# Sending 1536 columns of the upper 64 rows of one weight chunk to the lower partitions

## The reference, cut to what matters

```python
def _expert_choice_ffn(h, w_router, b_router, w_gate, w_up, w_down):
    ...
    gate, idx = lax.top_k(jnp.swapaxes(aff, 1, 2), cap)          # cap = 32 tokens for each of 16 experts
    xs = jax.vmap(lambda hb, ib: hb[ib])(h, idx)
    a = jnp.einsum('becd,edf->becf', xs, w_gate)                 # 1024 -> 2048
    u = jnp.einsum('becd,edf->becf', xs, w_up)                   # 1024 -> 2048
    y = jnp.einsum('becf,efd->becd', jax.nn.silu(a) * u, w_down) * gate[..., None].astype(h.dtype)
    ...                                                          # 2048 -> 1024, rows added back to their tokens
```

## Time and profile before

| | |
|---|---|
| median of 3 runs | 1540.61 us (1540.39 to 1540.74) |
| the profiled execution | 1540.27 us |
| its span | 1538.5 us, 18557 instructions |
| mean granted TensorE clock | 0.876 |
| busy PE / PEld | 78% / 45% |
| busy DVE / ACT / POOL | 40% / 28% / 2% |
| DMA | 550.12 MB, mean 358 GB/s |

### The profile page before, as it was taken

The page is one execution under the profiler, slowest core; times in us unless marked ns, Lnnn a source line. Parts: engine busy times, 40 slices in busy tenths (PEclk is TensorE's granted clock), DMA queues, the critical chain, the costliest instruction groups (busy, mean ns, idle before and its releaser), DMA issues.

```text
span 1538.5 us, 18557 instructions
## 1 busy us (share of the span) xinstructions
PE 1204.2 (78%) x7530; PEld 698.6 (45%) x7530; DVE 615.3 (40%) x1048; ACT 429.7 (28%) x652; POOL 35.5 (2%) x60
## 2 busy tenths in 40 slices
PE   9999999999999999987666566566565665665665
PEld 7888877887888899622111111111111111111112
DVE  5687789888777867511011011011011011011111
ACT  4665367786564664300000000000000000000001
POOL 0100000010001000000000000000000000000000
PEclk9999999999999999988777677877877777777788
DMA  9876876675755566999999999999999999999996
GB/s 384 323 271 229 299 269 245 227 284 197 284 183 199 219 239 274 409 435 429 433 430 430 433 431 429 432 432 429 429 436 428 429 436 426 432 435 425 434 434 281
DMA packets 40277, 550.12 MB, mean 358 GB/s; under 512 B 5001, under 2 KB 5289, under 8 KB 10497
## 3 DMA queue, kind: packets, MB, share of 16 engines
q1 hardware_dynamic: 37328, 541.08, 85.1%
q0 software_dynamic: 2576, 7.56, 1.5%
q10 hardware_dynamic: 288, 0.30, 0.1%
HBM read 547.84 MB, written 1.61 MB: 357 GB/s over the span
## 4 chain that ended last, share of the span: by engine, by line
PE 47%; DMA 34%; DVE 11%; ACT 3%; issue 3%; DVEq 0%; SPq 0%; ACTq 0%; POOL 0%
PE ps L671 45%; DMA b<-in_w_down 34%; DVE b L1636 5%; PE ps L675 3%; ACT b L1255 2%; DVE b L1653 2%; DVE b L2382 1%; DVE b L2323 1%; ACT b L1257 1%; DMA b<-in_dense 1%; DVE b L2329 1%; DVE b L2361 0%; DVE b L2363 0%; DVE b L1667 0%; ACT L1255 0%
## 5 line engine op out<-in xcount | busy, mean ns | idle before, releaser
L671 PE MATMUL ps<-b,b 128*32 128x512 f32 (+6 forms) x7070 | 1134.1, 536 | 288.0 <-DMA b<-in_w_up 113.3
L671 PEld LDWEIGHTS ps<-b,b 128*32 128x32 f32 (+2 forms) x7070 | 640.8, 158 | 742.5 <-issue 447.7
L1255 ACT ACTIVATE b<-ps 128x512 f32<-128x512 f32 (+4 forms) x169 | 93.4, 553 | 870.6 <-PE ps L671 571.8
L1636 DVE TENSOR_TENSOR b<-b,b 128x1024 fp32r<-128x1024 f32 (+5 forms) x254 | 277.1, 1091 | 95.2 <-ACT b L1255 76.8
L1255 ACT ACTIVATE b<-b 128x1024 fp32r<-128x1024 f32 (+6 forms) x219 | 219.1, 1000 | 191.7 <-PE ps L671 171.6
L2372 DVE TENSOR_TENSOR b<-b,ps 128x512 f32<-128x512 f32 x16 | 11.0, 689 | 391.4 <-issue 378.2
L2382 DVE TENSOR_TENSOR b<-b,ps 128x1024 f32<-128x1024 f32 x28 | 34.2, 1222 | 301.8 <-PE ps L671 301.8
L675 PE MATMUL ps<-b,b 128*128 128x128 f32 (+1 forms) x360 | 70.1, 322 | 37.3 <-DVE b L1667 22.9
L675 PEld LDWEIGHTS ps<-b,b 128*128 128x128 f32 (+1 forms) x360 | 45.8, 168 | 87.6 <-DVE b L1667 36.1
L1653 DVE SCALAR_TENSOR_TENSOR b<-b,b,b 128x512 f32<-128x512 f32 (+3 forms) x50 | 63.2, 1264 | 4.3 <-ACT b L1255 0.5
L1636 DVE TENSOR_TENSOR b<-ps,b 128x512 f32<-128x512 f32 (+8 forms) x73 | 38.3, 524 | 33.1 <-PE ps L671 14.3
(11 more groups left out here) (62 smaller groups left out, 204.2 us busy)
## 6 DMA issues: line engine op xcount, KB each, us to landing
b<-in_w_up SPq DMA_DIRECT2D x29, 4096.0 KB, 43.1
b<-in_w_down SPq DMA_DIRECT2D x29, 4096.0 KB, 38.3
b<-in_w_gate SPq DMA_DIRECT2D x28, 4096.0 KB, 42.9
b<-in_dense SPq DMA_DIRECT2D x88, 1024.0 KB, 5.3
b<-in_w_ada SPq DMA_DIRECT2D x24, 1024.0 KB, 6.9
b<-in_w_gate SPq DMA_DIRECT2D x6, 2048.0 KB, 10.1
b<-in_w_down SPq DMA_DIRECT2D x5, 2048.0 KB, 9.9
b<-in_ada SPq DMA_DIRECT2D x8, 1024.0 KB, 19.0
```

The costliest lines, as they stand in the source:

```text
L671: return e.matmul(o, lhsT, rhs, start=start, stop=stop, skip_group_check=True)
L1255: e.activation(o, i, f, bias=bias, scale=scale).then_inc(mark[0], 1)
L1636: e.tensor_tensor(o, a, b, op).then_inc(mark[0], 1)
```

## The change

Pair 45 is loaded by 25 transfers instead of one. The first brings columns 0 to 6655 of all 128 rows. The other 24 each bring eight rows: for i in (0, 1, 2, 3, 32, 33, 34, 35), rows i, i + 4, ..., i + 28 of the lower half with their columns 6656 to 8191 to their own place; and of the rows 64 higher, columns 6656 to 7167 into `HIGH2` and columns 7168 to 8191 into `HIGH3`, on the partitions of the lower rows. All of them count up `ew0`, so from then on all waits for this semaphore ask for 24 x 16 more.

These 1536 columns are the last three of the eight products of chunk 105 (b = 2 with nd = 1, b = 3 with both). Each of them becomes two products over 64 partitions: one with the lower half of `HTT` and the pair's buffer, one with `HTX` and `HIGH2` or `HIGH3`. `HTX` holds the upper 64 rows of `HTT[:, 2]` and `HTT[:, 3]` on the lower partitions. For that TensorE makes two more transposes, of columns 64 and on of `HD`'s parts, into bank 2, and ScalarE one more copy ahead of that to `HTT`; `a_ht` counts one more from expert 8 on.

```diff
--- before.py
+++ after.py
@@ -273,6 +273,10 @@
 E_ORDER = ("N", 16, 66, 0, 82, "HT", "ring2", 34, "ring0", "WS0", "WS2", 50, "N", 16)
 E_PAIR_AT = (66, "ring0", "WS0", 34, 0)
 
+E_UNEVEN = 8
+E_UNEVEN_PAIR = (E_UNEVEN * 12 + 8 - E_FIRST) // 2
+E_UNEVEN_PARTS = 25
+
 E_PAIR_FREE = (5, 9, 11, 12, 14)
 
 SCRATCH = 1024
@@ -436,6 +440,7 @@
 
         ACC, FG2, GG2, FJ = buf(HT_AT, NT, D), buf(HT_AT, NT, D), buf(HT_AT + 8, D), [buf(HT_AT + 12 + 2 * i, W) for i in range(2)]
         HD, HTT, YS = at(98, W), at(100, 4, P), at(102, W)
+        HIGH3, HIGH2, HTX = buf(HT_AT + 12, D), at(104, W), at(111, 2, P)
         AFFR, Z, XS, XT, GT = at(106, NT, P), at(107, NT, P), at(108, T), at(109, 2, P), at(110, T)
 
         junk = [at(106 + i, T) for i in range(4)]
@@ -500,7 +505,7 @@
             i = m % E_PAIRS
             if m == 1:
                 g = 1 - g
-            return EP[i][:, g * 4096:(g + 1) * 4096], (S(f"ew{i}"), 16 * (m // E_PAIRS + 2 + (i in E_TWICE)))
+            return EP[i][:, g * 4096:(g + 1) * 4096], (S(f"ew{i}"), 16 * (m // E_PAIRS + 2 + (i in E_TWICE) + (E_UNEVEN_PARTS - 1) * (m >= E_UNEVEN_PAIR and i == E_UNEVEN_PAIR % E_PAIRS)))
 
         def expert_half(n, b):
 
@@ -594,6 +599,14 @@
             def turned_load(n, k):
                 to, src = (v.rearrange("p (h k n) -> p h k n", h=2, k=2)[:, :, k, :] for v in (EW[n], chunk_src(n)))
                 e.dma_start(to, src).then_inc(S(f"ew{n}"), 16)
+
+            def uneven_pair(to, src, landed_):
+                e.dma_start(to[:, 0:6656], src[:, 0:6656]).then_inc(landed_, 16)
+                for i in (0, 1, 2, 3, 32, 33, 34, 35):
+                    low, high = slice(i, i + 32, 4), slice(64 + i, min(64 + i + 32, P), 4)
+                    e.dma_start(to[low, 6656:8192], src[low, 6656:8192]).then_inc(landed_, 16)
+                    e.dma_start(HIGH2[low, :], src[high, 6656:7168]).then_inc(landed_, 16)
+                    e.dma_start(HIGH3[low, :], src[high, 7168:8192]).then_inc(landed_, 16)
 
             e.wait_ge(S("p_half"), HALF_COUNT[next(g for g in range(NHALF) if HALVES[g][0:2] == (SLOT["G2"], 1))])
             turned_load(5, 0)
@@ -638,7 +651,9 @@
                     expert_load(n + 1)
                     continue
                 e.wait_ge(S("p_use"), E_PAIR_FREE[m] if m < E_PAIRS else n - 2 * E_PAIRS + 2)
-                if m < pairs - 1:
+                if m == E_UNEVEN_PAIR:
+                    uneven_pair(EP[i], pair_src(n), S(f"ew{i}"))
+                elif m < pairs - 1:
                     e.dma_start(EP[i], pair_src(n)).then_inc(S(f"ew{i}"), 16)
 
             e.dma_start(EP[i][:, 0:4096], chunk_src(n)).then_inc(S(f"ew{i}"), 16)
@@ -1115,6 +1130,11 @@
                 n = o.shape[-1]
                 return mm(o, HTT[:, b, 32 * j:32 * j + 32], w[:, b * D + c0:b * D + c0 + n], j == 0 and b < 2 and opens, j == 3 and b >= 2)
 
+            def down_uneven(w, b, nd, o):
+                high = HIGH3[0:64, nd * W:(nd + 1) * W] if b == 3 else HIGH2[0:64, :]
+                mm(o, HTT[0:64, b, 32:64], w[0:64, b * D + nd * W:b * D + (nd + 1) * W], False, False)
+                return mm(o, HTX[0:64, b - 2, 32:64], high, False, False)
+
             def down_last(w, j, b, nd):
 
                 for q in range(2):
@@ -1174,11 +1194,14 @@
                     gain_rows()
                 e.wait_ge(S("v_hd"), x + 1)
                 if x:
-                    e.wait_ge(S("a_ht"), x)
+                    e.wait_ge(S("a_ht"), x + (x > E_UNEVEN))
+                if x == E_UNEVEN:
+                    for b in (2, 3):
+                        flip(ps[0:64, 2, (b - 2) * P:(b - 1) * P], HD[:, 256 + b::4])
                 for b in range(4):
                     ins = flip(ps[:, 4, b * P:(b + 1) * P], HD[:, b::4])
                 ins.then_inc(S("p_ht"), 1)
-                e.wait_ge(S("a_ht"), x + 1)
+                e.wait_ge(S("a_ht"), x + 1 + (x >= E_UNEVEN))
                 if x == NE - 1:
 
                     for nd in range(2):
@@ -1198,6 +1221,8 @@
                             g = 2 * nd + b % 2
                             if x == NE - 1:
                                 ins = down_last(w, j, b, nd)
+                            elif (x, c) == (E_UNEVEN, 9) and 2 * b + nd >= 5:
+                                ins = down_uneven(w, b, nd, ps[32 * g:32 * g + 32, 5, :])
                             else:
                                 ins = down(w, j, b, ps[32 * g:32 * g + 32, 5, :], nd * W)
                     ins.then_inc(S("p_use"), 1)
@@ -1605,6 +1630,8 @@
                     e.wait_ge(S("v_hd"), x)
                 act(HD, ps[:, 2, :], ACT.Silu, to=S("a_sg"))
                 e.wait_ge(S("p_ht"), x + 1)
+                if x == E_UNEVEN:
+                    copy(HTX.rearrange("p a b -> p (a b)")[0:64, :], ps[0:64, 2, 0:T], to=S("a_ht"))
                 copy(HTT.rearrange("p a b -> p (a b)"), ps[:, 4, :], to=S("a_ht"))
                 if x == 0:
                     for n in range(2):
```

## The result

| | before | after |
|---|---|---|
| median of the runs on one chip | 1540.39 us (1540.17 to 1541.19, 21 runs) | 1542.94 us (1541.78 to 1544.3, 21 runs) |
| the profiled execution | 1540.27 us | 1542.46 us |
| its span | 1538.5 us | 1540.7 us |
| mean granted TensorE clock | 0.876 | 0.88 |

After / before is 1.0016, with a 95% interval of 1.001 to 1.0022: 2.55 us slower by the medians. The forecast was 1539.4 us, in a range of 1538.4 to 1542.8. The sign was wrong, and the median lies 0.14 us above the range. The result is about that of the first rival, "the late engines are (some of) the lower ones", whose price was 1542.6.

A forecast was written before the change was run, and what follows sets the result against it. The weight stream's last DMA engine was taken to bound the kernel. Relieving the late engines would end the stream at 1525.8 instead of 1527.0 us, 1.2 us earlier, all reaching the end: 1539.4 us against the median, range 1538.4 to 1542.8.

The forecast's parts named there:

- the first rival: Late DMA engines are some of the lower eight, so the end moves +2.0 us, up to 2.8, to 1542.6; chance 0.15.
- If the late eight are the upper ones: Stream's tail: late engines then end at 1525.2 us, one early-half engine at 1525.8, so the stream ends 1.2 us earlier.
- They go round eight engines: Instruction packets in the weight stream, about 1 us each, were read as passing through eight engines and making those late.
- What bounds the kernel: Expert stage: the DMA weight stream bounds it, and only the last of 16 engines to finish a transfer counts.
- Upper engines 1.83 us less, lower ones 2.0 more: Pair 45's load: 49,152 B move from each upper engine to a lower one; lower ends 1.8 and 2.8 us.
- 25 issues in 8 to 11 us: SP's issue of pair 45: 24 more at 0.33 to 0.47 us, hidden by data queued before pair 46; cost nothing.
- theory E: A theory of the follow-up experiments: SP's long issue of the small transfers holds the stream; no chance given.
- TensorE and ScalarE, nothing: Expert 8: 1.4 us more on TensorE, at most 0.60 on ScalarE, hidden by waits of 2.82 and 4.41 us.
- Fixed cost of a small transfer: Rival: each of 24 parts costs its engine fixed time; 1544.6 at 0.25 us; over 0.18 us or issue stall, chance 0.05.
- Spread over all sixteen: Rival: eight-row parts spread over all engines, nothing shifted, +0.2 us, 1540.8; chance 0.10 together with gain eaten.
- TensorE's waits: Sign to look for: waits for w_down and w_up fall little, as landings still come every 9.7 us.
- the stair at half height up to 1529: Sign in the tail's DMA share: a half-height stair reaching 1529 would say the late engines were the lower.

## Why the prediction was wrong

**The step that failed** is "If the late eight are the upper ones". They are mixed: six of the late ones are upper, two are lower, as the packet records at pair 45 show. By the prediction's own sizes all of the new tail follows: the six or so early lower engines 1521 + 2.0 = 1523, where the share leaves 0.94 (the step of 1522.5); late upper ones 1525.4 - 1.8 = 1523.6 and 1527.0 - 1.8 = 1525.2, where it falls through 0.5 to 0.2; late lower ones 1527.0 + 2.0 = 1529.0, where it becomes 0.00. Right sizes with the wrong owner. "One late engine among the lower eight is enough for this" was in the text, and it had 0.15.

The argument against it, "the stairs show exactly eight late ones, as a half would", was weak: eight of sixteen can be any eight. A share says how many engines work and not which. "They go round eight engines" agrees with the packet records (eight engines, six upper and two lower, as far as they can be followed), but nothing in it ties the eight to the partitions. The Trainium skill's rule on partitions ("DMA: Bandwidth & Descriptors", "The descriptor swizzle") doesn't either, and the text said so; the chance should have followed. With no evidence on the owner, "one of the lower eight is late" is far likelier than "all eight late ones are upper".

Point by point:

- *What bounds the kernel*: right. Only the last engine of the stream counts. Half the shift costs half (1.1 of 1.95 us), and the work beside the stream costs nothing that can be seen (1.0001 [0.9992, 1.001]).
- *Upper engines 1.83 us less, lower ones 2.0 more*: right within what half-microsecond steps show. At pair 45 the eight lower engines take 3.9 to 4.2 us from the start of the first small piece to the end of the last, where 3.87 was forecast.
- *25 issues in 8 to 11 us*: mis-sized. They took 19.1 us, 0.62 us for a transfer of eight rows, where 0.33 to 0.47 was taken from transfers of 128 rows. The cover named (data queued in front of pair 46) held: pair 46's issue came 1.2 us later, and the rate has no hole after it. For the change theory E falls with it; in the runs with 33 transfers for a pair it came true.
- *TensorE and ScalarE, nothing*: right, 1.0001 [0.9992, 1.001]. ScalarE's copies are 1.01 us for two instead of 0.60 for one, inside the bound. In the kernel after, though, the cover of 4.41 us shrank to 0.74, because pair 45 came later and its products ran partly at the lower clock; a little more and it would have been gone.
- *Fixed cost of a small transfer*: about none in the change (431 and 419 GB/s), and the 0.2 us for small packets was enough. The 2 us of the Trainium skill that the prediction set beside it ("DMA: Bandwidth & Descriptors", "Anatomy of one DMA") are given there for transfers that GpSimd issues; these come from SyncE, and no row shows such a cost. The price at 0.25 us was summed wrongly: 1525.8 + 24 x 0.25 is 1531.8, 4.8 us after 1527.0, so 1545.4 and not 1544.6.
- *Spread over all sixteen*: wrong for eight rows; the shift did take place, the 192 small packets are on eight engines. The Trainium skill's statement that eight rows run on the eight lowest engines ("DMA: Bandwidth & Descriptors", "Why a DMA increments its semaphore by 16 and not by 1") agrees with that as to their number; that they are the lowest, no record tells.
- *TensorE's waits*: w_up 112.8 and w_down 95.4 us, against 113.3 and 93.5; as forecast, hardly moved.
- *The result against the rival's price*: 2.55 us against 2.0 in the forecast. 1.95 are the transfers. What the other 0.6 are is open: the products alone cost 0.26 us by the medians, which is inside the noise, and the sum of the two is 2.2. The medians of the kernel before alone differ by 0.3 us between groups of runs.

Two sizes beside the main line were off as well. An instruction packet was taken at about 1 us, which left 28 of the 46 engine-us explained; with what it does to the next packet it is 1.55 us. And the smaller end of the gain, 0.5 us, is 0.4 by its own terms (1523.8 + 2.8 = 1526.6 against 1527.0).

A lesson on the "what would show it" part: it named the stair at half height up to 1529 as the sign of the rival. What came was a stair of an eighth up to 1529. The sign was right in its place and wrong in its height, for the same reason as the forecast.

## What to carry to other kernels

A stream that fills all sixteen DMA engines ends with its slowest engine. The stairs of the DMA share in the tail give the number of late engines and how late they are, but not which, and a shift of bytes is worth nothing unless every late engine is relieved: probe first with dummy transfers on a few engines, and look whether the last stair moves. Cut a wide transfer into pieces with care for the rows of each: pieces of all 128 rows cost nothing here, and eight neighbouring rows instead of every fourth cost 4.0 us for 0.8 MB. Count the issues, too: 24 small ones fitted in front of the data already queued, 32 didn't, and the stream ran dry behind them.

## What the hardware did that I had not expected

- The same columns of one pair cost nothing in pieces of 128 rows (1540.52 us), and 4.4 to 5.7 us in pieces of 4, 8, 16 or 64 rows in place or moved by halves. The rate falls to 210 to 323 GB/s for 10 us while all engines are busy. With eight rows in each transfer and a shift, the way the rows step decides: step four, 1542.39 us; neighbours, 1546.43.
- An issue of eight rows that step by four takes SP 0.62 us, one of eight neighbouring rows 0.30 us, one of 128 whole rows 0.33 us. So it isn't the small number of rows that makes an issue long. After some 20 to 24 small issues the next ones take up to 3.6 us.
- With 32 pieces of 2 KB in a row on each of the first four engines the first half takes 84 ns each and the second 162 to 179. With 16 pieces of 4 KB and eight of 2 KB between them there was no such loss (159 and 84 ns, nearly all). It isn't the columns read. What it is stays open.
- Eight engines lag by 4.5 to 6 us after a stream of 868 us. The instruction packets account for its size: 28 x 1.55 + 5 x 0.97 us is 48 engine-us against 46 in the stairs. No run took them away.
